# Clearing a phase's semaphores as one range, with the next phase on other numbers, in a two-block network on one core

## The reference

```python
def first_block(x, meta, ...):
    h = jnp.concatenate([meta, x], axis=1)
    for layer in range(DEPTH):
        h = h + 0.5 * swiglu_ffn(rms_norm(h, ffn_norm[layer, 0]), ...)
        hn = rms_norm(h, mix_norm[layer])
        if layer % 2 == 0:
            h = h + hybrid_attention_mixer(hn, ...)
        else:
            h = h + rwkv7_time_mix(hn, ...)
        h = h + 0.5 * swiglu_ffn(rms_norm(h, ffn_norm[layer, 1]), ...)
    return rms_norm(h, final_norm)[:, N_META:]

def second_block(x, ...):
    for l in range(DEPTH):
        mix = token_mixer(x, ...)
        x = layer_norm(DEEPNORM_ALPHA * x + mix, ln1_g[l], ln1_b[l])
        ffn = peer(x, ...)      # per token: top 16 of 8 heads, rows of peer_u and peer_v
        x = layer_norm(DEEPNORM_ALPHA * x + ffn, ln2_g[l], ln2_b[l])
    return x
```

## Time and profile before

| | us |
|---|---|
| median of 3 runs | 3826.02 |
| lowest, highest | 3821.34, 3834.89 |
| the profiled execution, own device time | 3831.39 |
| the profiled execution, span of its instructions | 3829.6 |
| PE busy | 3325.1 (87%) |
| DVE busy | 1659.5 (43%) |
| ACT busy | 700.2 (18%) |
| POOL busy | 602.1 (16%) |

### The profile page before, as it was taken

How to read it: one execution, slowest core, us unless ns; L and a number is a source line. 1 busy time by engine, 2 the same in 40 slices (tenths; PEclk the granted TensorE clock), 3 DMA queues, 4 the chain that set the end, 5 groups by cost and what they waited for, 6 DMA issues and landing times. The chain is left out here.

```text
span 3829.6 us, 47002 instructions
## 1 busy us (share of the span) xinstructions
PE 3325.1 (87%) x16666; PEld 2343.9 (61%) x16666; DVE 1659.5 (43%) x4102; ACT 700.2 (18%) x1530; POOL 602.1 (16%) x516
## 2 busy tenths in 40 slices
PE   8999679999989989989976888888799768787876
PEld 7876547878867968877865334333478653333432
DVE  2113441111164532111246766676312447676774
ACT  1100221111021211101222222222112312222222
POOL 0000000000000000000002444444100014444442
PEclk9999769999999989999988999999899889898999
DMA  4443013444422013443326999999534249999996
GB/s 171 147 153 110 2 43 118 148 155 142 149 81 89 4 42 125 157 150 130 124 100 249 421 421 422 421 422 422 207 134 153 77 187 421 421 422 414 421 421 254
DMA packets 113646, 828.08 MB, mean 216 GB/s; under 512 B 12528, under 2 KB 14064, under 8 KB 15120
## 3 DMA queue, kind: packets, MB, share of 16 engines
q0 software_dynamic: 73728, 536.90, 33.8%
q1 hardware_dynamic: 37184, 273.59, 19.3%
q10 hardware_dynamic: 2576, 15.59, 1.2%
HBM read 824.99 MB, written 1.05 MB: 216 GB/s over the span
## 5 line engine op out<-in xcount | busy, mean ns | idle before, releaser
L2471 PE MATMUL psum_all<-expert_rows,const_sb 128*128 128x512 f32 x2048 | 983.0, 638 | 243.9 <-ACT const_sb L2409 243.9
L2169 POOL DMA_INDIRECT expert_rows<-in_peer_uv_dram,head_experts x512 | 601.9, 1176 | 3173.6 <-issue 2161.8
L2471 PEld LDWEIGHTS psum_all<-expert_rows,const_sb 128*128 128x128 f32 x2048 | 408.9, 204 | 800.8 <-issue 480.2
L2287 DVE CUSTOM_DVE_ANT_0 expert_rows<-expert_rows,xn 128x1024 f32<-128x1024 f32 x512 | 616.8, 1224 | 285.1 <-DMA expert_rows<-in_peer_uv_dram,head_experts 280.7
L262 PE MATMUL psum_all<-xn,weight_ring 128*128 128x272 f32 (+1 forms) x3200 | 729.6, 391 | 0.0
L262 PEld LDWEIGHTS psum_all<-xn,weight_ring 128*128 128x128 f32 x3200 | 611.6, 191 | 117.8
L262 PE MATMUL psum_all<-hidden,weight_ring 128*128 128x272 f32 (+1 forms) x1408 | 318.6, 389 | 0.0
L262 PEld LDWEIGHTS psum_all<-hidden,weight_ring 128*128 128x128 f32 x1408 | 267.5, 190 | 50.5
L1842 PE MATMUL psum_all<-x,weight_ring 128*128 128x256 f32 x1024 | 229.9, 383 | 0.0
L2409 ACT ACTIVATE const_sb<-cst,head_weights 128x128 f32<-128x128 f32 x504 | 161.6, 392 | 326.2 <-DVE head_weights L2299 326.2
L1842 PEld LDWEIGHTS psum_all<-x,weight_ring 128*128 128x128 f32 x1024 | 193.5, 192 | 28.9 <-issue 2.9
(11 more groups left out here) (484 smaller groups left out, 3007.6 us busy)
## 6 DMA issues: line engine op xcount, KB each, us to landing
weight_ring<-in_ffn_in_dram SPq DMA_DIRECT2D x88, 1024.0 KB, 4.9
weight_ring<-in_w_in_dram SPq DMA_DIRECT2D x48, 1024.0 KB, 4.8
weight_ring<-in_ffn_out_dram SPq DMA_DIRECT2D x32, 1408.0 KB, 6.0
weight_ring<-in_peer_q_dram SPq DMA_DIRECT2D x16, 1024.0 KB, 9.1
weight_ring<-in_hyb_in_dram SPq DMA_DIRECT2D x12, 1024.0 KB, 4.9
wv<-in_w_v_dram ACTq DMA_DIRECT2D x8, 1024.0 KB, 6.3
weight_ring<-in_br_attn_dram SPq DMA_DIRECT2D x8, 1024.0 KB, 5.7
weight_ring<-in_br_lru_dram SPq DMA_DIRECT2D x8, 1024.0 KB, 5.8
```

What stands on the lines that cost most here:

```text
L2169: pool.indirect_dma_start(out=rows[:, j, :], out_offset=None, in_=a["peer_uv"], in_offset=bass.IndirectOffsetOnAxis(ap=idx[:, n, j:j + 1], ...
L2287: dve.tensor_tensor_reduce(row, row, xt[:, n, :], 1.0, 0.0, ALU.mult, ALU.add, dots[:, n, j:j + 1]).then_inc(S.dotted, 1)
L2471: mm = pe.matmul(sums(n, half), diag[:, j, :], rows[:, j, D + half * 512:D + (half + 1) * 512], start=False, stop=last and j == TOPK - 1)
```

## The change

Each phase now takes its semaphores from one of two fixed blocks of numbers, from 128 or from 192, in turn. At the end of a phase SP clears all of its own with one instruction over the range (L177 of the changed kernel), and after that each of the `shared` ones by itself (L179). The barrier that came behind the clears is gone, so the other engines go on into the next phase, which runs on the other block of numbers. A barrier stands ahead of a phase only where it shares a landed semaphore with the phase before it.

```diff
 def phase(nc, *names, shared=(), gathers=False):
+    names = ("act_step", "dve_step", "pool_step") + names
+    first = SEMS[TURN.n % 2]
+    used = range(first, first + len(names))
+    assert len(names) <= SEMS[1] - SEMS[0]
+    if set(shared) & set(TURN.shared):
+        nc.all_engine_barrier()
     with ExitStack() as ctx:
-        sems = {n: ctx.enter_context(nc.semaphore(n)) for n in ("act_step", "dve_step", "pool_step") + names}
+        sems = {n: ctx.enter_context(nc.semaphore(n, num=k)) for n, k in zip(names, used)}
         with nc.Block() as block:
             yield block, named(**sems)
         if gathers:
             nc.gpsimd.dma_reset()
             nc.all_engine_barrier()
-        for s in (*sems.values(), *shared):
+        nc.sync.sem_clear(used)
+        for s in shared:
             nc.sync.sem_clear(s)
-        nc.all_engine_barrier()
+        TURN.n, TURN.shared = TURN.n + 1, tuple(shared)
```

More of the change, by code:

```diff
@@ L145, in loop, with __init__ @@
         self.n = base + count * per
+class Turn:
+    def __init__(self):
+        self.n, self.shared = 0, ()
+TURN = Turn()
+SEMS = (128, 192)
 @contextmanager
 def phase(nc, *names, shared=(), gathers=False):
+    names = ("act_step", "dve_step", "pool_step") + names
[4 more added lines that the diff above has]
+        nc.all_engine_barrier()
     with ExitStack() as ctx:
-        sems = {n: ctx.enter_context(nc.semaphore(n)) for n in ("act_step", "dve_step", "pool_step") + names}
+        sems = {n: ctx.enter_context(nc.semaphore(n, num=k)) for n, k in zip(names, used)}
         with nc.Block() as block:
@@ L2638, in program @@
         w = Weights(nc, ctx)
+        TURN.n, TURN.shared = 0, ()
         psum_all = ctx.enter_context(nc.psum_tensor("psum_all", [P, 8 * 512], F32))
```

## The result

The changed kernel takes 3795.53 us (median of 4 runs, 3790.01 to 3802.02), the kernel before 3826.69 (4 runs). The ratio is 0.9917, with a 95% interval from 0.9891 to 0.9944. It is faster by 31.2 us. The forecast was 3788.3, 7.2 us lower, and the range 3777 to 3804.

A forecast was written before the change was run, and what follows sets the result against it. Most of the kernel was taken as PE-bound, about a third gather-bound, with seams paid by all. Seams 35.7 us plus clock 2 us gave 37.7 us off the 3826.0 us median: 3788.3 us, range 3777 to 3804.

The forecast's parts named there:

- The seams hold the gain, whatever bounds the phases: At the 28 seams between phases no engine computes; shortening them gains 35.7 us whatever bounds the phases beside them.
- 0.057 us for a clear: In the seams, each single clear costs 0.057 us; 499 leaving the path give 28.4 us, 30.6 with SP's pauses.
- 0.23 us for a barrier: In each seam the second barrier costs a fixed 0.23 us; 28 of them leaving the path give 6.5 us.
- A range clear at its lower bound: At phase ends, a range clear costs one single clear, 0.057 us; the upper bound would cost 5.0 us in all.
- Nothing late behind the seam: Behind the seams, engines and gathers all start earlier by the same amount; no earlier-issued transfer becomes a new stall.
- rivals A and B: Stalls entering next phase's code: A, 0.45 us pause per seam, 3800, chance 0.06; B, engines in a row, 3839, chance 0.03.
- Rival C: Only the seven norm seams pay, some 6 us, another wait replacing the seam elsewhere; 3820 us, chance 0.05.
- The clock, 2 us gained: Behind seams, shorter PE idle avoids some half-clock stretches: 2 us gained, between bounds of 5 gained and 2 lost.
- signs of being wrong: PE or DVE starting later than 0.1 to 0.5 us behind release, phases longer inside, or more 1.2 GHz stretches appearing than going.

The follow-up runs named there:

- single_beside: Changed kernel with every semaphore cleared by its own instruction again, beside the next phase, no barrier behind; 3785.9 us, ratio 0.9908 to the kernel before.
- no_cond: Changed kernel without the three barriers it keeps ahead of feed-forwards 1, 2 and 3; 3788.96 us, ratio 0.9907 to the kernel before.
- range_barrier: Changed kernel with the barrier behind the clears put back at the end of every phase, range clears kept; 3790.09 us, ratio 0.9931 to the kernel before.
- fill_ffn: Changed kernel with six products of constants behind PE's last matmul in the four feed-forwards alone; ratio 0.9936 to the kernel before.
- fill3: Changed kernel without its three kept barriers, with three products of constants behind PE's last matmul in ten phases; 3783.97 us, ratio 0.9888 to the kernel before.
- double_barrier: Kernel before the change with one more barrier of all engines behind the second one in all 28 seams; 3830.01 us, ratio 1.0026 to the kernel before.

## Why the prediction was right, point by point

- **The seams hold the gain, whatever bounds the phases** ("what it costs is paid by the whole kernel"): right. The seams lost 35.4 us, and 35.7 was the sum. The norm products wait 6.1 us less, as forecast. The first PEER phase starts its work 21.3 us earlier and lasts 1.3 us less. The seams ahead of it lost 22.7 us, the 23 that were forecast for its start; the other 1.4 went to the phases in between.
- **0.057 us for a clear**: right. In single_beside 82 clears more than in the changed kernel stood in front of somebody, 4.7 us by this price, and the seams grew by 5.0, or 0.061 each.
- **0.23 us for a barrier**: right for what the second barrier of the kernel before adds to its clears, too low for one by itself, which costs 0.33. The three kept ones with their clears cost 1.2 us in no_cond, as in the sum. That the whole came out so close (35.4 against 35.7) is no test of the split: both prices were read from the very seams that were summed, and range_barrier, which needs the split, missed by 3.3 us.
- **A range clear at its lower bound**: right. It takes 0.033 to 0.115 us, not up to 3.
- **Nothing late behind the seam**: nearly. No engine started later for want of the second barrier's cover. Counted from the last release ahead of it, the first instruction of PE, ACT and DVE comes as late as before wherever it waits for nothing: mostly 0.07 to 0.11 us, and 0.44 to 0.48 us for PE in the seams ahead of projections, in both kernels. SP's own first DMA of a phase comes 0.14 to 0.36 us behind the release instead of 0.07, for its clears. So rivals A and B fall. Rival C, 3820 us, falls with the measured time and with the work outside, which didn't take the seams' place: it grew by 2.4 us in the first trace and is 2352.9 on the mean of the four. A tile of weights in feed-forward 2 landed 2.0 us late in one trace of four, and about 1 us late in fill_ffn and fill3.
- **The clock, 2 us gained**: the term that failed, and no run shows it. In the profiled execution the work outside the seams is 2.4 us longer at the same time at half clock, of which 2.0 are the late tile, and PEER 1.9 longer. Over the four comparisons the gain is 32.6 us on the mean, 3 less than the seams give, and less than the spread of the four (25 to 37). Whether those 3 us are a loss at all is not shown: the work outside is 2358.9 and 2348.3 us in the two traces where the clears hold everyone up (before and double_barrier), and 2352.9 on the mean of the four of the changed kernel. The attention's 4.3 us are the one loss that came in each of the four, and even they were absent from no_cond. I had looked for the clock only behind the seams, where idle PE got shorter. But falls moved everywhere, and behind the six seams with a dense phase after them shorter idle of 2.0 to 2.5 us brought no clear change: 3 falls in the trace before, and 5, 1, 4 and 1 after. Two of the prediction's own signs of being wrong did show: phases longer inside, and 65 stretches at half clock in place of 63 (63, 66 and 64 in the other traces).
- **Luck in the number**: that the time at half clock came out equal in the first pair of traces is chance. The RWKV mixer's first phase took 151.6 us before and 143.8 after, with 21.9 and 5.1 us at half clock. It took 143.9 in double_barrier too, where the clears hold everyone up as before, so the change didn't bring this gain. It hid losses elsewhere, the attention's among them. The mechanism was right and gives the 35.4 us. The clock's 2 us were a guess between bounds of 5 gained and 2 lost, and it did not come true.

## What to carry to other kernels

Where phases are cut by barriers, let the housekeeping of one phase (clearing semaphores) run beside the next on another set of numbers, and keep a barrier only where the two share something; price each seam from release to release and multiply, since here it was paid ahead of PE's phases and of the gathers' alike. Check such a change by the sum of its seams in the trace: here that was 7.1 us in all four traces, where the gain in the kernel's time lay anywhere from 25 to 37 us. Don't read an effect of the clock from one trace: at equal idle time a fall came in about half of the cases (28 of 58). Shortening PE's idle time from three microseconds to two and a half didn't clearly help (3 falls behind the six seams before, and 5, 1, 4 and 1 after). Shortening it to 0.3 to 0.8 us made the falls right behind a seam rare (1 of 14), but no gain in the kernel's time was shown for it.

## What the runs showed of the hardware that I had not expected

- A range clear costs almost nothing for each number more. In the changed kernel the clear of the last norm's 5 numbers takes 33 ns and that of the first PEER phase's 52 takes 109 ns, 1.6 ns a number:

```profile
L177 SPq EVENT_SEMAPHORE_RANGE_CLEAR  x1: 33/33/33, 1659.8 to 1659.8; - x1
...
L177 SPq EVENT_SEMAPHORE_RANGE_CLEAR  x1: 109/109/109, 2725.8 to 2725.8; - x1
```

- A barrier of five engines that all stand ready costs 0.33 us, one behind a row of clears on one of them 0.23 us more than the clears at 0.057 us each.
- One kernel's executions differ by up to 17 us in the phases that PE bounds, mostly through where the clock stands at half clock: 28.6 us more of busy PE at that clock went with 15.4 us more time, once the late tile is taken off.
- The clock can fall behind idle times of PE of only 2.0 to 3.3 us, and does so in about half of the cases (28 of 58), at the same seam in one execution and not in the next.
